# Taking the 128-byte spacer between the two weight rings out, and putting it ahead of the activations

## What is computed

```
proj = x @ w_in
...
h = layer_norm(DN_ALPHA * h + mix, ...)
h = layer_norm(DN_ALPHA * h + jnp.square(jax.nn.relu(h @ w_up)) @ w_down, ...)
...
yff = (jax.nn.silu(u_g) * u_v) @ w_down[l]
x = x + _rms_norm(yff, norm_ffn_post[l])
```

## Time and profile before

| | |
|---|---|
| median of 3 runs | 1233.64 us (1231.74 to 1233.78) |
| the profiled execution | 1233.64 us, of which 1231.8 us are the span from its first to its last instruction |
| TensorE, matmuls | busy 1199.4 us, 10380 matmuls |
| TensorE, weight loads | busy 1164.4 us |
| VectorE | busy 869.0 us |
| ScalarE | busy 669.1 us |
| granted TensorE clock, mean | 0.993 of 2.4 GHz |

### The profile page before, as it was taken

How to read it: one execution, slowest core, us unless ns; L and a number is a source line. 1 busy time by engine, 2 the same in 40 slices (tenths; PEclk the granted TensorE clock), 3 DMA queues, 4 the chain that set the end, 5 groups by cost and what they waited for, 6 DMA issues and landing times.

```text
span 1231.8 us, 24532 instructions
## 1 busy us (share of the span) xinstructions
PE 1199.4 (97%) x10380; PEld 1164.4 (95%) x10380; DVE 869.0 (71%) x1383; ACT 669.1 (54%) x879; POOL 39.4 (3%) x30
## 2 busy tenths in 40 slices
PE   9989999999999999999999999999999999999997
PEld 8868999999989999999999999989999999999997
DVE  6777966466856588645676544879988766999843
ACT  6445553454466345534435558675465566777741
POOL 0331000000000000000000001000000000000000
PEclk9999999999999899999999999999999999999999
DMA  8223256455458223654642559965445432655430
GB/s 363 92 85 125 88 215 223 171 186 224 147 155 224 103 103 139 237 184 161 236 171 76 209 193 280 282 198 198 152 167 204 171 134 73 221 189 204 171 138 35
DMA packets 30770, 213.34 MB, mean 173 GB/s; under 512 B 3672, under 2 KB 4184, under 8 KB 5336
## 3 DMA queue, kind: packets, MB, share of 16 engines
q1 hardware_dynamic: 27792, 195.83, 43.5%
q0 software_dynamic: 2016, 14.68, 5.9%
q10 hardware_dynamic: 872, 1.54, 0.4%
HBM read 210.99 MB, written 1.05 MB: 172 GB/s over the span
## 4 chain that ended last, share of the span: by engine, by line
PE 82%; DVE 9%; ACT 5%; issue 2%; DMA 2%; DVEq 0%; ACTq 0%
PE lin L520 23%; PE lin L521 23%; PE lin L522 23%; ACT whi L1266 2%; PE lin L550 2%; DMA raw<-units_dram 2%; PE lin L557 2%; PE lin L551 2%; PE lin L663 1%; PE att L656 1%; DVE wlo L1833 1%; PE lin L700 1%; PE att L852 1%; DVE pr L1974 1%; DVE work L2104 1%
## 5 line engine op out<-in xcount | busy, mean ns | idle before, releaser
L520 PE MATMUL lin<-xh,whi 128*128 128x256 f32 x1712 | 478.1, 279 | 2.6 <-DVE amax L2119 1.1
L522 PE MATMUL lin<-xh,wlo 128*128 128x256 f32 x1712 | 473.9, 277 | 0.0
L521 PE MATMUL lin<-xl,whi 128*128 128x256 f32 x1712 | 473.9, 277 | 0.0
L1833 DVE TENSOR_TENSOR wlo<-raw,whi 128x2048 fp32r<-128x2048 f32 x165 | 377.0, 2288 | 133.7 <-ACT whi L1266 133.1
L1266 ACT ACTIVATE whi<-raw 128x2048 fp32r<-128x2048 f32 x183 | 349.4, 1911 | 157.7 <-PE lin L522 141.9
L520 PEld LDWEIGHTS lin<-xh,whi 128*128 128x128 f32 x1712 | 322.6, 188 | 6.1 <-issue 4.4
L521 PEld LDWEIGHTS lin<-xl,whi 128*128 128x128 f32 x1712 | 322.6, 188 | 0.6 <-issue 0.5
L522 PEld LDWEIGHTS lin<-xh,wlo 128*128 128x128 f32 x1712 | 322.4, 188 | 0.0
L520 PE MATMUL lin<-fh,whi 128*128 128x256 f32 x512 | 141.7, 277 | 0.0
L522 PE MATMUL lin<-fh,wlo 128*128 128x256 f32 x512 | 141.3, 276 | 0.0
L521 PE MATMUL lin<-fl,whi 128*128 128x256 f32 x512 | 141.3, 276 | 0.0
(11 more groups left out here) (402 smaller groups left out, 1919.3 us busy)
## 6 DMA issues: line engine op xcount, KB each, us to landing
raw<-units_dram SPq DMA_DIRECT2D x183, 1024.0 KB, 4.8
wlo<-units_dram POOLq DMA_DIRECT2D x14, 1024.0 KB, 13.2
h<-x_dram SPq DMA_DIRECT2D x1, 1024.0 KB, 6.9
out_dram<-h SPq DMA_DIRECT2D x4, 256.0 KB, 2.0
consts<-consts_dram SPq DMA_DIRECT2D x1, 864.0 KB, 15.8
narrow_a<-narrow_a_dram SPq DMA_DIRECT2D x1, 544.0 KB, 8.8
aqT<-mem_dram ACTq DMA_DIRECT2D x1, 512.0 KB, 6.0
fkT<-mem_dram ACTq DMA_DIRECT2D x1, 512.0 KB, 6.9
```

The costliest lines, as they stand in the source:

```text
L520: mm(out, w[0], a[0], start=first, stop=False)
L521: mm(out, w[0], a[1], start=False, stop=False)
L522: return mm(out, w[1], a[0], start=False, stop=last)
L1833: v.tensor_tensor(wlo[u % RING][:], raw[u % RING][:], whi[u % RING][:].bitcast(f32), ALU.subtract).then_inc(lo_ready, 1)
```

## The change

The spacer `between_w` (32 float32, 128 bytes) is taken out, and `ahead_of_x` grows by as much. So `wlo0` to `wlo3`, `h` and `z` start 128 bytes earlier than before; `raw`, `whi`, `xh` and everything behind it stay where they were. No instruction is added, removed or moved to another place in its queue.

```diff
         raw = [sbuf(f"raw{i}", [P, UW]) for i in range(RING)]
         whi = [sbuf(f"whi{i}", [P, UW], f32r) for i in range(RING)]
-        sbuf("between_w", [P, 32])
         wlo = [sbuf(f"wlo{i}", [P, UW], f32r) for i in range(RING)]
         h = sbuf("h", [P, DB, S])
         z = sbuf("z", [P, DB, S])
-        sbuf("ahead_of_x", [P, 16])
+        sbuf("ahead_of_x", [P, 48])
         xh = sbuf("xh", [P, DB, S], f32r)
         xl = sbuf("xl", [P, DB, S], f32r)
```

## The result

The changed kernel took 1240.1 us, the median of 8 runs (1237.34 to 1244.54), against 1233.86 us for the kernel before on the same chips (8 runs, 1231.74 to 1236.22): ratio 1.0066, 95% interval 1.0044 to 1.0090. It is slower by more than can be told from no change, and outside the predicted range. The third rival came about in part: the clear pace is lost in some of the long stretches, not in all. In all, 28 executions of the changed kernel were timed, from 1237.34 to 1249.15 us with a median of 1242.2 us; the eight lie low among them, and the ratio is nearer to the 28 (1242.2 / 1233.86 = 1.0068) than to the eight (1.0051). The profiled execution took 1242.54 us, in the middle of the 28, with a span of 1240.7 us, 8.9 us more than before. Sums over its trace are therefore some 2.7 us larger than the difference of the two medians of eight (6.2 us).

The account below looks back on a forecast made before the run. TensorE was taken as the bound, with matmuls busy for 97% of the span. Terms of -1.35, -0.2 and +0.5 summed to -1.05 us, from 1233.64 to 1232.6 us; the range was 1228.0 to 1235.2.

Parts of the forecast that it names:

- The third rival: Long xh, fh, gh stretches lose the clear pace without alternating distances; 42 us more, 1275 us at the worst; chance 0.14.
- the clear pace: TensorE's shorter step between 128x256 matmul starts, 0.1133 us, read from the last MLP; longer steps were called held up.
- the distance of the two streams: Address of the moving tensor less that of the weights being loaded, modulo 256; claimed to govern TensorE's pace.
- Nothing changes: Rival: the two paces depend on something other than the distance; 1233.6 us, chance 0.17.
- once they have slipped apart they stay so, whatever the distances: Claim that TensorE's moving stream and weight loads, once no longer colliding, keep the clear pace at any distance.
- (a): Distance 192 throughout, xh, fh, gh moving or weights over mhi: clear within about four steps; 1.35 and 0.2 us less.
- The point from which it decides (450): Held-up matmuls, less than ten units, at which a loss of the clear pace outweighs 2.5 us.
- (b): Distance 64 throughout, bhi and mhi moving and weights over xh: a steady 0.1183 us a step, 0.5 us more.
- distance 64 settles as well: Rival: any uniform distance lets the streams slip apart, so 64 becomes clear too; 1228.6 us, chance 0.24.
- (c): VectorE and ScalarE writing wlo at its new address: at most 2.3 us of VectorE, taken as 0.
- (d): DMA: raw landings, additions into wlo and the final store of h at new addresses; taken as 0.

Follow-up runs that it names:

- the probe: A kernel of matmuls only, sixteen pairs of distances between moving tensor and loaded weights, six stretches each; 113.3 to 121.1 ns a step.
- swapped: The kernel before with wlo declared ahead of whi, so the two weight rings change places; 1237.54 us, ratio 1.0021.
- no_spacers: The kernel before with both spacers, between the weight rings and ahead of xh, taken out; 1273.87 us, ratio 1.0349.
- branches_shifted: The kernel before with 128 bytes put in ahead of the branch and cross attention tensors, so bhi and mhi come to 192; 1231.93 us, ratio 0.9987.
- the second probe: The same matmul-only kernel with 23 cases, some begun by 24 matmuls at 192/64; 192 alone clear in two of six stretches, behind turns in six.
- after_again: The changed kernel run once more with no edit; 1248.13 us, one run.
- wlo_alone: Only wlo moves by 128 bytes, h and z stay where the kernel before had them; 1248.3 us, ratio 1.0116.
- hz_alone: The kernel before with only h and z moved to the remainders modulo 256 of the changed kernel; 1233.72 us, ratio 0.9994.
- after: The changed kernel in its first profile; the profiled execution took 1242.54 us.
- after_mixed: The changed kernel plus eight unread matmuls at 192 and 64 by turns, behind the last MLP's unit_first; 1242.3 us, ratio 1.0069.

## Why the prediction was wrong, point by point

- **What sets the pace.** That the step of a 128x256 matmul follows from the distance of the two streams modulo 256, and not from other engines, held: the probe has it with nothing else running, 448 behaves as 192 does, and `swapped`, `no_spacers` and `branches_shifted` came in at the paces of their distances. "Nothing changes" is out. But "once they have slipped apart they stay so, whatever the distances" did not hold: in the second probe the clear pace was lost at 64 and at 0, in six of six stretches each.
- **(a), the step that failed.** "So at uniform 192 the clear pace comes within about four steps." Expected was 1.55 us less; measured in the trace 10.5 us more (2.77 to 13.25). I inferred it from L557 in the earlier trace rows, where four steps at 192 clear a held-up stretch. In that kernel every such stretch comes directly behind matmuls that had 192 and 64 by turns; what was held up there was the pattern of the turns (steps of 117 to 123 ns, 120 in the mean), not the steady 117.8 ns that 192 has by itself. The probes show what that hid: behind turns, which were clear by their end, 192 alone is clear in six of six stretches, behind a stop in two of six. The individual places where I looked for (a) came out as predicted, and this is worth seeing. Timeline of PE of the changed kernel, the start of the first unit_first and the unit of the earlier trace rows:

```profile
15.48 0.28 PE L550 MATMUL lin<-xh,wlo 128*128 128x256 f32 x1
15.60 0.28 PE L549 MATMUL lin<-xh,whi 128*128 128x256 f32 x1
15.72 0.28 PE L550 MATMUL lin<-xh,wlo 128*128 128x256 f32 x1
15.84 0.28 PE L549 MATMUL lin<-xh,whi 128*128 128x256 f32 x1
15.95 0.28 PE L550 MATMUL lin<-xh,wlo 128*128 128x256 f32 x1
16.06 0.28 PE L549 MATMUL lin<-xh,whi 128*128 128x256 f32 x1
...
731.49 0.28 PE L520 MATMUL lin<-xl,whi 128*128 128x256 f32 x1
731.61 0.29 PE L521 MATMUL lin<-xh,wlo 128*128 128x256 f32 x1
731.73 0.28 PE L519 MATMUL lin<-xh,whi 128*128 128x256 f32 x1
731.85 0.28 PE L520 MATMUL lin<-xl,whi 128*128 128x256 f32 x1
731.96 0.28 PE L521 MATMUL lin<-xh,wlo 128*128 128x256 f32 x1
```

  The first leaves 0.12 us a step for 0.11 after three steps while it still alternates, the second is clear from its fifth step. They are outcomes that fell well. Part of the gain that I counted is there (unit_firsts 1.09 to 0.69 us), but it isn't safe: they stand at 1.23 us in `after_again` and at 1.46 in `wlo_alone`. What I left out is that a stretch that misses the clear pattern in its first steps now misses it to its end, and one end is 1552 steps away.
- **The rival that came.** "The two distances by turns might be what pushes the streams apart in the long stretches." That was right. That "192 alone can fall back" was not: the held-up long stretch did not lose the clear pace, it never reached it. Its price was not right either: I let 7600 steps fall back by 5.5 ns (42 us); in the trace (8.64 + 1.48 + 2.21 us) / 4.45 ns = 2770 of 7100 steps were held up, 1330 / 4.45 = 300 before. The point from which it decides (450) was passed more than five times over. The argument against it was "after L557 every unit stays clear", which holds at 192, as the probe's stretches behind turns show, but is no answer to a stretch that never was clear.
- **(b) Distance 64.** A steady pace without the 283 ns matmuls came: the groups of PE from 866 to 875 us have 280, 279 and 279 ns:

```profile
L520 PE MATMUL lin<-blo,whi 128*128 128x256 f32 x25 | 7.0, 280 | 0.0
L519 PE MATMUL lin<-bhi,whi 128*128 128x256 f32 x25 | 7.0, 279 | 0.0
L521 PE MATMUL lin<-bhi,wlo 128*128 128x256 f32 x25 | 7.0, 279 | 0.0
```

  It is 117.8 ns, where I had 118.3. With that (b) lies 0.37 us under before instead of 0.5 us above it. Most of that comes from one place: the first 96 steps of the units that make `av` (from 680.50 us), which follow clear `xh` matmuls without a stop, ran clear at distance 64. The 192 steps with `xh` that follow them without a stop, at 192, were held up (0.1178), where the kernel before was clear within a few steps; `after_again` has the same three pieces with the same paces. So a change of roles in a running stretch decides anew as well, and not by the pace ahead of it. The probe never has the clear pace at 64 alone, so "distance 64 settles as well" is out but for this place.
- **(c), (d).** Nothing, as predicted. `wlo` as an output at remainder 0, the row of the changed kernel against 2288 ns in the earlier trace rows:

```profile
L1832 DVE TENSOR_TENSOR wlo<-raw,whi 128x2048 fp32r<-128x2048 f32 x165 | 377.1, 2289 | 135.7 <-ACT whi L1265 135.0
```

  `raw` lands in 4.8 us, the additions into `wlo` in 13.2 and the store in 2.0, all as in the earlier trace rows; `hz_alone` made no difference.
- **The chances.** I gave the rival 0.14 with a range that left it out. The prediction looked for its weak place in the length of L557's stretches; it was in what stands ahead of them, and the test for it was in the trace of before: no stretch there begins at uniform 192. So nothing in the rows spoke for the forecast in such a stretch, and the two outcomes had earned about the same weight.

**What stays open.** What in the first steps behind a stop picks the pattern is not settled. It isn't pure chance: the six stretches at 192 came out in the same order in both probes (clear, held up, clear, then three held up), those of 448 in that order too, and those of 64/192 alternate in both. In the kernel it goes largely with what stands ahead. I took the four traces with 192 alone (`after`, `after_again`, `wlo_alone`, `after_mixed`): the stretches that begin behind the matmul with `zsum` (256 columns) are held up in 14 of 16 cases, those behind a matmul of `pT` with `gate` (128 columns) in 4 of 32, and these four are the same one of the eight each time. The six stretches of a case in the probes differ in how long ScalarE's work ahead of them is and, in the last three, in the matmuls of 128 columns ahead, so when and behind what a stretch begins is what I suspect; no run varied that by itself. In the kernel that moment can shift with every wait, which would make the rest of it a draw. Nor do the runs show where inside TensorE or SBUF the two streams meet. Whether eight matmuls by turns would rescue the changed kernel's long stretch isn't known, because the run drew a clear one.

## What to carry to other kernels

Where TensorE is the bound and weights are loaded for every matmul, look at the step between starts, not at busy shares, and compare it over stretches of one shape; here 113.3 against 117.8 ns is 4%, and the place of the tensors decides which paces can come. A pattern that keeps itself must be judged by what a stretch starts from: evidence from stretches that enter it from another state says nothing of stretches that begin in it. And a change that makes the outcome a draw costs more than its mean: the 28 executions of the changed kernel spread over 11.8 us, the 20 of the kernel before that were timed beside the first experiments over 4.6. The clock alone doesn't explain that: 1249.15 us had a mean clock of 0.997, 1237.86 us one of 0.991.

## What the runs showed that was not expected

- Sixteen bytes count. In the second probe one distance of 176 gave 119.3 ns and 208 gave 119.2 (one stretch 116.7), on either side of 192 with its 113.3 or 117.8.
- 96/224 by turns is the worst pair at 121.1 ns, 7% above the clear pace. Two uniform distances, 0 and 96, are at 120.0.
- The kernel without spacers had a granted clock of 0.999 over its span, where before had 0.993; its program outside the measured steps was 9.4 us shorter.
- With 64/192 in the kernel, the stretches of over 1000 steps were all clear, while some 20 of the shorter stretches ran at 118.9 ns in whole or in part; the probe had three and three. Two paces for one pair of distances are thus not special to 192 alone.
